# Moving the store and the fetch of the hidden tile in a SwiGLU weight stream, with its split and the row sums moved too

## The reference

```python
def swiglu_ffn(x, norm_pre, w_gate, w_up, w_down, norm_post):
    h = rms_norm(x, norm_pre)
    a = jax.nn.silu(jnp.einsum('bsd,df->bsf', h, w_gate)) * jnp.einsum('bsd,df->bsf', h, w_up)
    y = jnp.einsum('bsf,fd->bsd', a, w_down)
    return x + rms_norm(y, norm_post)
```

## Time and profile before

| | |
|---|---|
| median of 3 runs | 1983.43 us (1980.13 to 1987.91) |
| profiled execution, its time | 1980.94 us |
| profiled execution, its span | 1979.2 us |
| TensorE busy | 1942.5 us, 98% of the span |
| VectorE busy | 1609.1 us, 81% |
| ScalarE busy | 1122.0 us, 57% |
| GpSimd busy | 245.0 us, 12% |
| HBM traffic over the span | 205 GB/s |
| TensorE granted clock | 0.998 of full speed |

### The profile page before, as it was taken

The page is one execution under the profiler, slowest core; times in us unless marked ns, Lnnn a source line. Parts: engine busy times, 40 slices in busy tenths (PEclk is TensorE's granted clock), DMA queues, the critical chain, the costliest instruction groups (busy, mean ns, idle before and its releaser), DMA issues.

```text
span 1979.2 us, 26465 instructions
## 1 busy us (share of the span) xinstructions
PE 1942.5 (98%) x9598; PEld 1643.2 (83%) x9598; DVE 1609.1 (81%) x2100; ACT 1122.0 (57%) x1428; POOL 245.0 (12%) x145
## 2 busy tenths in 40 slices
PE   9999999999999999999999999999999999999998
PEld 7898878778778888888899988788787788888886
DVE  5755578898889868788699986688998998788797
ACT  6544465555555545455778875465555555545554
POOL 1000000000000000000489940000000000000000
PEclk9999999999999999999999999999999999999999
DMA  9645556666666766666455545556666666766564
GB/s 342 229 142 191 178 167 227 212 217 223 220 223 227 241 226 211 210 193 203 143 192 180 183 137 192 165 192 228 213 223 223 213 218 231 254 211 208 188 216 154
DMA packets 138010, 408.12 MB, mean 206 GB/s; under 512 B 15330, under 2 KB 38498, under 8 KB 137378
## 3 DMA queue, kind: packets, MB, share of 16 engines
q1 hardware_dynamic: 135796, 396.84, 60.3%
q0 software_dynamic: 2096, 9.70, 1.3%
HBM read 392.84 MB, written 13.63 MB: 205 GB/s over the span
## 4 chain that ended last, share of the span: by engine, by line
PE 59%; DVE 25%; DMA 9%; SPq 3%; issue 3%; ACT 1%; POOL 0%; DVEq 0%; ACTq 0%; POOLq 0%
PE acc L1840 39%; DVE w_lo L1165 9%; DMA raw<-in_units 9%; PE acc L1851 4%; PE acc L1853 4%; PE acc L1852 4%; DVE gate_sum_lo L1461 3%; PE acc L2030 2%; PE acc L2031 2%; PE acc L2032 2%; SPq L555 2%; DVE gpost L1442 2%; DVE raw L1448 2%; DVE gpost L1449 2%; DVE gpost L1455 1%
## 5 line engine op out<-in xcount | busy, mean ns | idle before, releaser
L724 ACT ACTIVATE w_hi<-raw 128x1024 fp32r<-128x1024 f32 x632 | 657.6, 1056 | 684.9 <-DVE raw L1448 293.4
L1165 DVE TENSOR_TENSOR w_lo<-raw,w_hi 128x1024 fp32r<-128x1024 f32 x546 | 650.9, 1219 | 164.5 <-ACT w_hi L724 163.3
L1840 PE MATMUL acc<-w_hi,xT_hi 128*128 128x512 f32 x1112 | 344.3, 391 | 3.3 <-DVE w_lo L1167 2.7
L1840 PE MATMUL acc<-w_lo,xT_hi 128*128 128x512 f32 x1112 | 342.6, 389 | 0.0
L1840 PE MATMUL acc<-w_hi,xT_lo 128*128 128x512 f32 x1112 | 342.4, 389 | 0.0
L1840 PEld LDWEIGHTS acc<-w_hi,xT_hi 128*128 128x128 f32 x1112 | 207.5, 188 | 49.2 <-DVE w_lo L1167 3.7
L1840 PEld LDWEIGHTS acc<-w_lo,xT_hi 128*128 128x128 f32 x1112 | 208.7, 188 | 43.6
L1840 PEld LDWEIGHTS acc<-w_hi,xT_lo 128*128 128x128 f32 x1112 | 208.8, 188 | 43.5
L1851 PE MATMUL acc<-xT_hi,w_hi 128*128 128x256 f32 x640 | 181.3, 283 | 0.0
L1853 PE MATMUL acc<-xT_hi,w_lo 128*128 128x256 f32 x640 | 181.1, 283 | 0.0
L1852 PE MATMUL acc<-xT_lo,w_hi 128*128 128x256 f32 x640 | 181.1, 283 | 0.0
(11 more groups left out here) (283 smaller groups left out, 3105.8 us busy)
## 6 DMA issues: line engine op xcount, KB each, us to landing
raw<-in_units SPq DMA_DIRECT2D x702, 512.0 KB, 4.1
hid_turned_blocks<-tok SPq DMA_DIRECT2D x44, 256.0 KB, 2.1
tok<-hid_turned_blocks SPq DMA_DIRECT2D x176, 64.0 KB, 2.7
gpost<-in_post POOLq DMA_DIRECT2D x4, 1024.0 KB, 6.8
x<-in_x POOLq DMA_DIRECT2D x4, 512.0 KB, 8.9
c_raw<-in_consts POOLq DMA_DIRECT2D x4, 512.0 KB, 7.0
out<-x SPq DMA_DIRECT2D x8, 256.0 KB, 2.8
xT_raw<-in_xT SPq DMA_DIRECT2D x3, 512.0 KB, 7.2
```

The lines of the kernel that those rows point to most:

```text
L724: nc.scalar.activation(w_hi[:, s, :], raw[:, s, :], ACT.Copy, scale=scale).then_inc(hi_ready, 1)
L1165: ins = nc.vector.tensor_tensor(w_lo[:, s, :], raw[:, s, :], w_hi[:, s, :], ALU.subtract)
L1840: last = mm(acc[:, 4 * par + 2 * t + h, :], xs, ws[:, s, h * BANK:(h + 1) * BANK], start=start and ws is w_hi and xs is xh, stop=stop and ...
```

## The change

- `tok` gets another layout: the inner tile of both tokens in its first half (`inner`), the turned tile in its second half (`turned_inner`); before, each token had a half with both.
- The store is one transfer for both tokens, behind all of quad 2's loads. The fetch is four transfers, each with 32 partitions of both tokens, between units 1 and 2 of quad 3. One semaphore each serves both tokens.
- ScalarE's `hi_hid` of token 0 and 1 stand behind its units 2 and 3 of quad 3; VectorE's `lo_hid` likewise.
- VectorE joins the rows ahead of unit 3 of chunk 1's quad 0, and sums them behind it; ScalarE rounds them behind `silu`.
- GpSimd's remainder of unit 3 of quad 0 stays as it was.

```diff
@@ fetched
         def fetched(t):
-            return tok[:, t * DA:t * DA + BANK].rearrange("p (i k b) -> p k i b", k=4, b=32)
+            return inner(t).rearrange("p (i k b) -> p k i b", k=4, b=32)
@@ SyncE
                 for t in range(T):
                     sp.wait_ge(hid_turned[t], i + (FFC * layer + 1))
-                    sp.dma_start(d_hid[t], tok[:, t * DA + BANK:(t + 1) * DA]).then_inc(hid_stored[t], 16)
+                src = tok[:, DA:].rearrange("p (t n) -> p t n", t=T)
+                sp.dma_start(d_hid.rearrange("t p n -> p t n"), src).then_inc(hid_stored, 16)
 
             def fetch_hidden(i, layer):
-                for t in range(T):
-                    sp.wait_ge(hid_stored[t], i * 16 + (FFC * layer + 1) * 16)
-                    src = d_hid[t].rearrange("(i a) (q n) -> q a i n", a=32, n=P)
-                    for quadrant in range(4):
-                        dst = tok[32 * quadrant:32 * (quadrant + 1), t * DA:t * DA + BANK].rearrange("p (i n) -> p i n", n=P)
-                        sp.dma_start(dst, src[quadrant]).then_inc(hid_fetched[t], 16)
+                sp.wait_ge(hid_stored, i * 16 + (FFC * layer + 1) * 16)
+                src = d_hid.rearrange("t (i a) (q n) -> q a (t i) n", a=32, n=P)
+                for quadrant in range(4):
+                    dst = tok[32 * quadrant:32 * (quadrant + 1), 0:DA].rearrange("p (i n) -> p i n", n=P)
+                    sp.dma_start(dst, src[quadrant]).then_inc(hid_fetched, 16)
...
-                    load_quad(i * 4 + (q0 + 2), pool, (0, 1, 2))
+                    load_quad(i * 4 + (q0 + 2), pool)
                     store_hidden(i - 1, layer)
-                    load_quad(i * 4 + (q0 + 2), pool, (3,))
+                    load_quad(i * 4 + (q0 + 3), pool, (0, 1))
                     fetch_hidden(i - 1, layer)
-                    load_quad(i * 4 + (q0 + 3), pool)
+                    load_quad(i * 4 + (q0 + 3), pool, (2, 3))
@@ ScalarE, split_fast
-                    split(q, 2)
-                    split(q, 3)
+                    for s in (2, 3):
+                        split(q, s)
+                        if inner is not None:
+                            hi_hid(inner, s - 2)
@@ ScalarE, ffn
-                hi_rows(rows + 1, xs_hi[:], gate_raw_sum.rearrange("p (a c) -> p a c", c=BANK))
                 for i in range(1, FFC):
                     q = i * 4 + q0
                     split_quad(q, *(gain, 0) if i == 1 else ())
                     silu(i - 1, 0)
                     silu(i - 1, 1)
+                    if i == 1:
+                        hi_rows(rows + 1, xs_hi[:], gate_raw_sum.rearrange("p (a c) -> p a c", c=BANK))
...
-                        if c == 2:
-                            hi_hid(i - 1, 0)
-                            hi_hid(i - 1, 1)
+                                if c == 3 and s >= 2:
+                                    hi_hid(i - 1, s - 2)
@@ VectorE, end of open_ffn
                 split(q + 3, 3)
-                dve.wait_ge(xT_lo_ready, parted(b, 1, 3))
-                dve.wait_ge(x_scaled, len(RESCALED) * (e // 2) + 1)
-                dve.wait_ge(y_gained, 8 * e + 8)
-                join_rows(gate_raw_sum, first_tiles(xT_hi, 4, 3), first_tiles(xT_lo, 4, 3), 3)
-                sum_rows(gate_raw_sum, 3, (1 + len(SUM_BATCHES)) * (e // 2) + 1)
@@ VectorE, ffn
                     if i == 1:
+                        dve.wait_ge(xT_lo_ready, parted(e, 1, 3))
+                        dve.wait_ge(x_scaled, len(RESCALED) * layer + 1)
+                        dve.wait_ge(y_gained, 8 * e)
+                        join_rows(gate_raw_sum, first_tiles(xT_hi, 4, 3), first_tiles(xT_lo, 4, 3), 3)
                         split(q, 3, gain + 3)
+                        sum_rows(gate_raw_sum, 3, rows + 1)
...
                     if 3 in fast:
                         begin_sums(q + 3, gate_sum(layer, i, 3), gate_raw_sum)
-                        lo_hid(i - 1, 0)
                         sum_corner(q + 3, gate_raw_sum)
-                        lo_hid(i - 1, 1)
                         end_sums(q + 3, gate_raw_sum)
-                    else:
-                        lo_hid(i - 1, 0)
-                        lo_hid(i - 1, 1)
...
                     split(q + 3, 2)
+                    lo_hid(i - 1, 0)
                     split(q + 3, 3)
+                    lo_hid(i - 1, 1)
```

More of the change, by code:

```diff
@@ L384, in trunk @@
         hid_turned = [sem(f"hid_turned{t}") for t in range(T)]
-        hid_stored = [sem(f"hid_stored{t}") for t in range(T)]
-        hid_fetched = [sem(f"hid_fetched{t}") for t in range(T)]
+        hid_stored = sem("hid_stored")
+        hid_fetched = sem("hid_fetched")
         hT_hi_ready = sem("hT_hi_ready")
@@ L473, in first_tiles, with inner, turned_inner @@
             return hi[:, k:k + 4 * n, :].rearrange("p (a k) c -> p a (k c)", k=4)[:, :, 0:BANK]
+        def inner(t):
+            return tok[:, t * BANK:(t + 1) * BANK]
+        def turned_inner(t):
+            return tok[:, DA + t * BANK:DA + (t + 1) * BANK]
         def fetched(t):
-            return tok[:, t * DA:t * DA + BANK].rearrange("p (i k b) -> p k i b", k=4, b=32)
+            return inner(t).rearrange("p (i k b) -> p k i b", k=4, b=32)
         def by_token(hT, i, t):
@@ L901, in silu, with split_fast @@
                         src = acc[:, private_bank(par, t, 0), :]
-                    nc.scalar.activation(tok[:, t * DA + BANK:(t + 1) * DA], src, ACT.Silu,
+                    nc.scalar.activation(turned_inner(t), src, ACT.Silu,
                                          scale=x_rs[:, t:t + 1]).then_inc(silu_ready, 1)
                 def hi_hid(i, t):
-                    act.wait_ge(hid_fetched[t], i * 64 + (FFC * layer + 1) * 64)
+                    act.wait_ge(hid_fetched, i * 64 + (FFC * layer + 1) * 64)
                     nc.scalar.activation(by_token(hT_hi, i, t), fetched(t), ACT.Copy).then_inc(hT_hi_ready, 1)
-                def split_fast(q, n, raw_sum, rescale=False):
+                def split_fast(q, n, raw_sum, rescale=False, inner=None):
                     act.wait_ge(raw_corner_ready, n)
@@ L938, in ffn @@
                     silu(i - 1, 1)
+                    if i == 1:
+                        hi_rows(rows + 1, xs_hi[:], gate_raw_sum.rearrange("p (a c) -> p a c", c=BANK))
                     for c in range(1, 4):
                         if c in fast_quads(i):
-                            split_fast(q + c, gate_sum(layer, i, c), gate_raw_sum, i == 1 and c == 2)
+                            split_fast(q + c, gate_sum(layer, i, c), gate_raw_sum, i == 1 and c == 2, i - 1 if c == 3 else None)
                         else:
@@ L1415, in hidden @@
                     up = parts[:, 2 * t + 1, :] if i in FAST_CHUNKS else acc[:, private_bank(par, t, 1), :]
-                    nc.vector.scalar_tensor_tensor(tok[:, t * DA:t * DA + BANK], up, x_rs[:, t:t + 1],
-                                                   tok[:, t * DA + BANK:(t + 1) * DA], ALU.mult, ALU.mult).then_inc(hid_ready, 1)
+                    nc.vector.scalar_tensor_tensor(inner(t), up, x_rs[:, t:t + 1],
+                                                   turned_inner(t), ALU.mult, ALU.mult).then_inc(hid_ready, 1)
                 def turn_hidden(i, t):
                     dve.wait_ge(hid_ready, i * 2 + (22 * layer + t + 1))
-                    nc.vector.transpose(tok[:, t * DA + BANK:(t + 1) * DA],
-                                        tok[:, t * DA:t * DA + BANK]).then_inc(hid_turned[t], 1)
+                    nc.vector.transpose(turned_inner(t),
+                                        inner(t)).then_inc(hid_turned[t], 1)
                 def lo_hid(i, t):
```

## The result

The changed kernel takes 1969.62 us (median of 6 runs, 1966.12 to 1974.82) where the kernel before takes 1982.78 (6 runs): a ratio of 0.9934, with a 95% interval of 0.9914 to 0.9954. That is 13 us faster, where 27.7 were forecast. The time lies in the stated range, but far from the forecast's 1955.7.

What follows compares the result with a forecast made beforehand. TensorE, busy 98%, was taken as the bound, so only its waits and lost pace could be won: 25.2 at quad 3 plus 2.5 at chunk 1, 27.7 us, giving 1953.2, as a median 1955.7 us; range 1949 to 1974.

Steps and rivals of the forecast that it cites:

- step 3: VectorE per fast chunk: 38.4 us of work plus waits of 1.05 and 0.75, together 40.2, under TensorE's 41.48 by 1.3.
- The second rival: Quad 3's loads slowed by surrounding transfers: loss from a 5.85 us landing, about half the gain at 6.6; chance 0.13.
- the ring: VectorE's work and waits for loads in a fast chunk, which must fit into TensorE's 41.48 us.
- Steps 2 and 7: Quad 3: `lo_hid` out of the sums, 1.2 us less before slot 0's remainder; chunk 1: row sums moved, 2.5 us.
- step 7: Opening of chunk 1 in both layers: waits of 0.98 and 0.97 us go, 1.26 per layer, 2.5 together.
- step 1: Quad 3 of fast chunks: slot 1's load leaves at 402.9, not 405.62, so VectorE begins the sums 2.7 us earlier.
- Steps 4 and 6: Store behind quad 2's last load, landing in 2.1 to 4.1 us; `hi_hid` moved into quad 3: nothing on the path.
- step 6: `hi_hid` behind quad 3's slots 2 and 3: a fetch lands 2.7 us from issue, at most 5.2; nothing on the path.
- Step 5: Four fetches for eight: issues take 1.7 us, up to 3.5; slot 2 of quad 3 is used late, cost nothing.
- The slower rival: SyncE waits at the fetch for the store's landing, holding later loads: 2003.7 us as a median; chance 0.04.

Runs made afterwards that it cites:

- two halves: The changed kernel with the fetch as two transfers of 64 partitions, in 2 KB pieces: 0.9911 of the kernel before.
- long pieces: The changed kernel with the four fetch transfers in 256 pieces of 2 KB in place of 1024 of 512 B: 0.9936 of the kernel before.
- the first experiment: The changed kernel with the fetch behind all four of quad 3's loads: 0.9973 of the kernel before.

## Why the prediction was wrong in its size

**The step that failed** is the first, by the size of one term: slot 1's load, "with the same 4.55 us it lands at 407.5". Its start was right (at once behind its remainder), but the landing was carried over from a load that stood behind the fetch to one that stands ahead of it. It measured 6.3 us (median). I had argued that the load, now ahead of the fetch, would be the better for it. A load that is issued 0.37 us ahead of the fetch isn't protected from it: without the fetch it takes 4.45, with it as one wide transfer 5.5, as four narrow ones 6.05 to 6.3.

**A second term failed, the margin of step 3.** By its 1.3 us a chunk, 1.75 us of later landing would have cost 0.45 us a chunk, about 8 us in 17; some 14 of the 27.7 us stayed away. The sum of 40.2 took VectorE's busy time and the two waits for loads, but in the earlier trace rows VectorE is idle 42.93 - 38.41 = 4.52 us, and its waits for loads in that stretch are only 4.1:

```profile
DVE gpost L1442 <- DMA raw<-in_units: 4.1, 2, 3.0
```

The other 0.4 us were left out. With them the margin is 0.9, and without the fetch it measures 0.8.

**The mechanism was right, the threshold was not.** The second rival named this case, with 5.85 us as the landing at which the ring is full. With the measured margin it is full at 4.45 + 0.8, about 5.3 us (an estimate from the run without the fetch); 5.5 us still cost next to nothing, 5.8 did cost. The estimate fits the chunks of the changed kernel: where landings average 6.3 us (the six chunks of layer 0) they take 0.9 us too many, and where they average 6.7 (the seven of layer 1) 1.36. The profiled executions, by the landing of slot 1, take 1951.66 us (4.45, no fetch), 1951.61 (5.5, one wide), 1962.73 (5.8, two halves), 1963.68 (5.9, eight fetches), 1958.39 (6.0, no store), 1963.42 (6.05, long pieces) and 1970.50 (6.3). From 5.8 us on they lose, though not evenly. The rival's 1969.5 us was worked out for a landing of 6.6: at 6.3 its own rule gives 1953.2 + 17 x 0.45, about 1961, or 1963 as a median. The match is luck, a threshold too high and a landing too late. The chance of 0.13 was too small. The row of 6.08 us already said how far such a load can go with a fetch beside it; I took it for an outlier.

**Steps 2 and 7 were no gains of their own.** Moving `lo_hid` by itself gives 1.0011, moving the row sums 0.9999. Where VectorE's work and its two waits fill a chunk, taking 1.2 us from ahead of quad 3 only adds it behind, and what TensorE wins at the opening it waits for at the next quad 3. Added to the sum, the 2.5 us of step 7 were right only because step 1 was to make TensorE the bound. Taken together with the queue's change they are no loss: without the fetch the whole forecast sum comes out (0.9864, and 1951.66 us against 1953.2).

**Step 3 was right in its two waits and its outcome,** wrong in its margin: without the fetch, with 0.66 and 1.02 us of waits in place of 0.75 and 1.05, VectorE waits at `add_parts`, as forecast.

**Steps 4 and 6 cost nothing on the path,** as forecast: the store of 512 KB lands in 2.8 us (median), inside the bounds of 2.1 and 4.1, and the tile is in time. It comes later than step 6 said, though: a fetch lands in 5.6 us (median), not 2.7. Step 5 had the price of the issues nearly right (1.91 us for four, 1.7 taken) and was right that slot 2 has room (it lands in 6.9 us in place of 4.1, and nothing waits), but looked only at the queue. What four transfers in 1.9 us do to the load ahead of them wasn't priced; eight would have been better, 0.9872.

**The slower rival** didn't occur, but its kind did in the first experiment: a fetch moved back by some 4 us more held ScalarE for up to 3.8 us, and with it the ring. The Trainium skill's advice in "DMA: Bandwidth & Descriptors", section "Rules for kernel authors", to issue a transfer early and wait late, fits this trace: 0.9973 with the fetch late and its readers in place, 0.9854 with the readers late as well.

**What stays open:** how the load and the fetch share the DMA engines. A wide fetch adds 1.05 us and the narrow form about 0.6 more; pieces of 2 KB in place of 512 B change little (6.05 and 6.3). Why a wide fetch hurts where a load of as many bytes didn't, and whether the width of a transfer or their number counts, wasn't separated. The Trainium skill says in "SBUF — State Buffer", section "Can I just issue two DMAs to hit both halves?", that only one transfer over all 128 partitions reaches all ports of the memory; the order of the landings here (6.05, 5.8 and 5.5 us for four, two and one transfer) agrees with it without proving it.

## What to carry to other kernels

When an engine's work and its waits for loads add up to nearly the time of a loop, sum them per turn of the loop, against the bound engine's time: moving that engine's work about gives nothing, only a shorter wait or less work does. A load on the path is priced by what is issued next to it on both sides, behind it too; put other transfers where the load has landed, in front of loads that have time to spare, and move their readers as far back as the transfer. Take the idle time in such a sum whole (the stretch less the busy time), not as the waits that one has spotted: here the margin was 0.8 us and not 1.3. And look at the spread of the rows that it rests on, not only at their middle.

## What the runs showed of the hardware

- A load of 512 KB, issued 0.37 us ahead of a transfer of 512 KB in four parts of 32 partitions each, lands in 6.3 us; with nothing behind it for 2.8 us it lands in 4.4, and with another load of 512 KB 0.5 us behind it, in the kernel before, in 4.5. Pieces of 2 KB in place of 512 B make 6.05 of the 6.3, one transfer over 128 partitions 5.5.
- Eight transfers of 64 KB hold that load no more than four of 128 KB (5.9 and 6.3 us) and give the better time, though their issue takes twice as long (3.65 and 1.91 us).
- VectorE's subtraction of two SBUF tiles waits when GpSimd works on two others: 128 x 512 took 2.41 us in place of 0.68 beside GpSimd's 2.40, and three remainders 5.69 in place of 3.49. The Trainium skill's "SBUF — State Buffer", section "Who interferes with whom", says that a VectorE instruction with two inputs in SBUF contends with a GpSimd instruction that reads SBUF, and that the order of issue decides which of the two is blocked; the trace agrees, as VectorE's starts 0.54 us later than GpSimd's and its 2.41 us end at 423.74, 0.55 after GpSimd's.
- In the changed kernel TensorE's granted clock fell to half, the level of 1.2 GHz, from 1422.0 to 1425.4, behind its longest wait (2.08 us, ahead of 1421.20). Ten matmuls were under way in that stretch and 16 in the next of the same length:

```profile
1422.00:1425.40 3.40, 3.40 (x10) 2.63 (x9) 3.40 (x4) 3.40 (x7) 0.00 (x0) 0.50 0.87 267
1425.40:1428.80 3.40, 3.40 (x16) 2.80 (x15) 3.33 (x6) 2.04 (x3) 0.00 (x0) 1.00 0.75 218
```

  In the kernel before it didn't fall behind the wait of 2.81 us. TensorE has no wait at the next quad 3, so it isn't shown that this made the changed kernel longer.
